# Latent attention's value products: a rounded part and a remainder side by side in one stationary tile, on one Trainium2 core

## The reference, cut to what matters

```python
    def attend(qblk):
        s = jnp.einsum('bqhd,bkhd->bhqk', qblk, k).astype(jnp.float32)
        p = jax.nn.softmax(s, axis=-1)
        return jnp.einsum('bhqk,bkhd->bqhd', p.astype(v.dtype), v)

    o = lax.map(attend, qb)
    o = o.transpose(1, 0, 2, 3, 4).reshape(B, S, B_HEADS * V_DIM)
    return o @ w_o
```

## Time and profile before

| | |
|---|---|
| median of 3 runs | 1272.54 us (1271.21 to 1272.92) |
| profiled execution, first to last instruction (span) | 1270.8 us |
| profiled execution, its own time | not given apart from its span |
| PE matmul busy | 1201.8 us, 95% of the span |
| DVE busy | 634.5 us, 50% |
| ACT busy | 370.1 us, 29% |
| POOL busy | 432.6 us, 34% |
| mean granted TensorE clock | 0.987 of full speed |
| dense attention, first scores to last values | 652.9 to 853.6 us |

### The profile page before, as it was taken

One profiled execution on the slowest core, in us unless ns is written; L12 is line 12 of the kernel. 1 busy time (PEld: TensorE's weight loads), 2 busy tenths in 40 slices (PEclk: granted clock), 3 DMA queues, 4 the chain that ended last, 5 costly groups with the idle time before them and its releaser, 6 DMA issues.

```text
span 1270.8 us, 19309 instructions
## 1 busy us (share of the span) xinstructions
PE 1201.8 (95%) x5804; PEld 996.6 (78%) x5804; DVE 634.5 (50%) x1055; ACT 370.1 (29%) x719; POOL 432.6 (34%) x474
## 2 busy tenths in 40 slices
PE   6988899999999999999989899999999999999996
PEld 4777787878888888888967677777788888888885
DVE  6666674444432544445476767745433432343432
ACT  3167672232210011011165656532222200101101
POOL 5455543433321323334242314215333321333341
PEclk9999999999999999999999999999999999999998
DMA  6211012233333233332201001013323432333331
GB/s 158 67 35 33 17 34 67 84 99 99 90 109 98 85 98 89 106 114 88 76 18 36 19 17 33 1 34 116 99 83 99 117 93 80 92 98 99 109 90 66
DMA packets 176473, 96.62 MB, mean 76 GB/s; under 512 B 8753, under 2 KB 173105, under 8 KB 176433
## 3 DMA queue, kind: packets, MB, share of 16 engines
q1 hardware_dynamic: 176432, 96.12, 25.9%
HBM read 94.01 MB, written 2.10 MB: 76 GB/s over the span
## 4 chain that ended last, share of the span: by engine, by line
PE 78%; DVE 8%; issue 6%; POOL 3%; ACT 3%; DMA 1%; DVEq 0%; ACTq 0%; SPq 0%; POOLq 0%
PE bank L975 25%; PE bank L977 24%; PE bank L976 24%; PE bank L1419 2%; POOL w_hi L436 1%; PE bank L1116 1%; DVE stat L2010 1%; POOL bias L516 1%; DVE w_lo L1501 1%; DMA w_raw<-in_a_w_qkv 1%; DVE bpt_lo L2015 1%; DVE apt_lo L1672 0%; ACT s_b L906 0%; DVE k_dup L1592 0%; DVE w_lo L1518 0%
## 5 line engine op out<-in xcount | busy, mean ns | idle before, releaser
L1501 DVE TENSOR_TENSOR w_lo<-w_raw,w_hi 128x1024 fp32r<-128x1024 f32 (+2 forms) x151 | 202.9, 1344 | 294.5 <-POOL w_hi L436 294.4
L436 POOL TENSOR_SCALAR w_hi<-w_raw 128x1024 fp32r<-128x1024 f32 (+3 forms) x159 | 184.5, 1160 | 414.8 <-PE bank L977 404.3
L975 PE MATMUL bank<-x_hi,w_lo 128*128 128x512 f32 x784 | 309.2, 394 | 8.4 <-DVE w_lo L1501 5.3
L976 PE MATMUL bank<-x_lo,w_hi 128*128 128x512 f32 x784 | 306.9, 391 | 0.0
L977 PE MATMUL bank<-x_hi,w_hi 128*128 128x512 f32 x784 | 306.6, 391 | 0.0
L975 PEld LDWEIGHTS bank<-x_hi,w_lo 128*128 128x128 f32 x784 | 147.9, 189 | 41.6 <-DVE w_lo L1501 7.4
L977 PEld LDWEIGHTS bank<-x_hi,w_hi 128*128 128x128 f32 x784 | 148.2, 189 | 31.4
L976 PEld LDWEIGHTS bank<-x_lo,w_hi 128*128 128x128 f32 x784 | 148.2, 189 | 29.4
L975 PE MATMUL bank<-f_hi,w_lo 128*128 128x512 f32 x352 | 137.8, 391 | 1.1 <-DVE f_lo L1782 1.1
L977 PE MATMUL bank<-f_hi,w_hi 128*128 128x512 f32 x352 | 137.0, 389 | 0.0
L976 PE MATMUL bank<-f_lo,w_hi 128*128 128x512 f32 x352 | 137.0, 389 | 0.0
(11 more groups left out here) (215 smaller groups left out, 1946.9 us busy)
## 6 DMA issues: line engine op xcount, KB each, us to landing
w_raw<-in_ffn_w_gu SPq DMA_DIRECT2D x88, 512.0 KB, 3.8
w_raw<-in_ffn_w_down SPq DMA_DIRECT2D x32, 704.0 KB, 4.4
w_raw<-in_a_w_qkv SPq DMA_DIRECT2D x12, 512.0 KB, 3.7
w_raw<-in_a_w_o SPq DMA_DIRECT2D x8, 512.0 KB, 3.5
w_raw<-in_b_w_o SPq DMA_DIRECT2D x8, 512.0 KB, 3.8
w_raw<-in_b_w_in SPq DMA_DIRECT2D x4, 672.0 KB, 4.0
w_raw<-in_b_w_uq SPq DMA_DIRECT2D x4, 576.0 KB, 4.0
x_n<-in_x SPq DMA_DIRECT2D x4, 512.0 KB, 5.0
```

The lines of the kernel that those rows point to most:

```text
L436: pool.tensor_scalar(split_part(w_hi, s, cols, kv), raw_part(s, cols, kv), 1.0, 1.0, ALU.mult, ALU.mult) \
L975: pe.matmul(o, ll, rh, start=start, stop=False)
L976: pe.matmul(o, lh, rl, start=False, stop=False)
L1501: dve.tensor_tensor(split_part(w_lo, s, cols, kv), raw_part(s, cols, kv), f(split_part(w_hi, s, cols, kv)), ALU.subtract) \
```

## The change

The value tile `bv` now holds, for each head and key block, the 64 columns of the rounded values and beside them the 64 columns of the remainder. A head takes two matmuls a key block, this tile x `bpt_lo` and this tile x `bpt_hi`. In the bank, partitions 0 to 63 then hold the rounded values' share and 64 to 127 the remainder's share (with low x low, which was left out before); their sum is the head's output. Heads 0 to 2 of a group use bank 5, head 3 bank 2. Per head ACT copies the lower half to `o_low` (`o_lower`) and DVE adds it to the upper half into a half of `o_sum` (`o_total`). After each odd head DVE copies `o_sum` to `ot_hi`, and POOL makes `ot_lo` from `o_sum` and `ot_hi` (`o_split`). `o_hi`, `o_lo` and the two memsets of the zero columns are gone. `wo_phase` waits for POOL's `o_ready` in place of DVE's `o_free`. The diff, its core:

```diff
@@ -201,11 +201,11 @@
             ("bk_hi", [P, HG, T], F32R), ("bk_lo", [P, HG, T], F32R)])
-        cq_hi, cq_lo, ckv_hi, ckv_lo, q_n, bv_hi, bv_lo, s_b, bpt_hi, bpt_lo, rope_a = region(scratch, [
+        cq_hi, cq_lo, ckv_hi, ckv_lo, q_n, bv, o_low, o_sum, s_b, bpt_hi, bpt_lo, rope_a = region(scratch, [
             ("cq_hi", [P, QL // P, T], F32R), ("cq_lo", [P, QL // P, T], F32R),
             ("ckv_hi", [P, KVL // P, T], F32R), ("ckv_lo", [P, KVL // P, T], F32R),
             ("q_n", [P, NT, HG * QK], F32),
-            ("bv_hi", [P, NT, 2, 3 * HD], F32R), ("bv_lo", [P, NT, 2, 3 * HD], F32R),
+            ("bv", [P, NT, HG, 2 * HD], F32R), ("o_low", [HD, T], F32), ("o_sum", [P, T], F32),
             ("s_b", [P, 2, HG, T], F32),
@@ -618,6 +620,14 @@
+            pool.memset(o_sum[:, 0:2], 0.0).then_inc(o_ready, 1)
+            def o_split(g, pair):
+                wait(pool, o_hi_ready, 4 * GROUPS + 2 * g + pair + 1)
+                pool.tensor_tensor(ot_lo[:, 2 * g + pair, :], o_sum[:], f(ot_hi[:, 2 * g + pair, :]), ALU.subtract) \
+                    .then_inc(o_ready, 1)
@@ -629,6 +639,9 @@
                         w_split_hi(C_B // 2 + 1 + g, 1, cols1, kv=cols0 == W_UQ)
+                    if u == 15:
+                        o_split(g, 0)
+                o_split(g, 1)
@@ -860,14 +873,12 @@
-            bv_hi_v = bv_hi[:].rearrange("p t a (s d) -> p (t a) s d", d=HD)
             def b_v_hi(g, i):
-                wait(act, o_done, 4 * GROUPS + 2 * g)
+                wait(act, o_done, 4 * GROUPS + HG * g)
                 wait(act, proj_done, U_BG * g + 6 + i + 1)
-                act.activation(bv_hi_v[:, 4 * i:4 * i + 4, ::2, :],
-                               banks[6 + i][:].rearrange("p (t s d) -> p t s d", t=4, s=2), ACT.Copy) \
+                act.activation(bv[:, 2 * i:2 * i + 2, :, 0:HD],
+                               banks[6 + i][:].rearrange("p (t h d) -> p t h d", t=2, h=HG), ACT.Copy) \
                     .then_inc(v_hi_ready, 1)
@@ -911,9 +920,11 @@
-                def o_hi(pair):
-                    wait(act, o_done, 4 * GROUPS + 2 * g + pair + 1)
-                    act.activation(ot_hi[:, 2 * g + pair, :], banks[5][:], ACT.Copy).then_inc(o_hi_ready, 1)
+                def o_lower(n):
+                    wait(act, o_free, O_B + HG * g + n)
+                    wait(act, o_done, 4 * GROUPS + HG * g + n + 1)
+                    act.activation(o_low[:], banks[5 if n < 3 else 2][HD:P, :], ACT.Copy).then_inc(o_low_ready, 1)
@@ -936,8 +947,8 @@
                             pt_hi(n, i)
-                        if n == 2:
-                            o_hi(0)
+                        if n:
+                            o_lower(n - 1)
                     else:
@@ -946,10 +957,11 @@
                                 b_k_hi(g + 1, i // 2)
+                        o_lower(2)
                         if not last:
                             for hd in range(HG):
                                 b_q_hi(hd, T_B + B_TG * g + 16)
-                        o_hi(1)
+                        o_lower(3)
@@ -1001,7 +1013,10 @@
                     pe.wait_ge(proj_free, u0 + s - 1)
-                    pe.wait_ge(o_free, O_A + 4 * (GROUPS - 1) if c0 == C_WOA else O_B + 2 * (GROUPS - 1))
+                    if c0 == C_WOA:
+                        pe.wait_ge(o_free, O_A + 4 * (GROUPS - 1))
+                    else:
+                        pe.wait_ge(o_ready, 2 * (GROUPS - 1) + 1)
                 for k in ks:
@@ -1196,9 +1211,9 @@
-            def wo_phase(c0, u0, o_count):
-                pe.wait_ge(o_free, o_count)
+            def wo_phase(c0, u0, o_landed, o_count):
+                pe.wait_ge(o_landed, o_count)
                 for s in range(2):
@@ -1405,6 +1420,8 @@
                     pe.wait_ge(exp_ready, S_B - S_A + before)
+                    if u == 2:
+                        pe.wait_ge(o_free, O_B + HG * g)
                     q = (slice(0, QK), n, slice(qb * P, (qb + 1) * P))
@@ -1431,14 +1448,14 @@
                             pe.wait_ge(proj_free, U_B + U_BG * g + U_BG)
-                    if i == 0 and n % 2 == 0:
-                        pe.wait_ge(o_free, O_B + 2 * g + n // 2)
-                    v = (slice(None), i, n // 2, slice(HD, HD + P) if n % 2 else slice(0, P))
-                    p = (slice(None), n % 2, i, slice(None))
-                    last_ = product(banks[5][:], bv_hi[v], bv_lo[v], bpt_hi[p], bpt_lo[p],
-                                    n % 2 == 0 and i == 0, n % 2 == 1 and i == NT - 1)
-                    if n % 2 and i == NT - 1:
+                    if i == 0 and n < 3:
+                        pe.wait_ge(o_free, O_B + HG * g + n)
+                    o = banks[5 if n < 3 else 2][:]
+                    v = bv[:, i, n, :]
+                    pe.matmul(o, v, bpt_lo[:, n % 2, i, :], start=i == 0, stop=False)
+                    last_ = pe.matmul(o, v, bpt_hi[:, n % 2, i, :], start=False, stop=i == NT - 1)
+                    if i == NT - 1:
                         last_.then_inc(o_done, 1)
@@ -1968,14 +1983,11 @@
-            bv_hi_v = bv_hi[:].rearrange("p t a (s d) -> p (t a) s d", d=HD)
-            bv_lo_v = bv_lo[:].rearrange("p t a (s d) -> p (t a) s d", d=HD)
             def b_v_lo(g, i):
                 wait(dve, v_hi_ready, GROUPS + 2 * g + i + 1)
-                dve.tensor_tensor(bv_lo_v[:, 4 * i:4 * i + 4, ::2, :],
-                                  banks[6 + i][:].rearrange("p (t s d) -> p t s d", t=4, s=2),
-                                  f(bv_hi_v[:, 4 * i:4 * i + 4, ::2, :]), ALU.subtract).then_inc(proj_free, 1)
+                dve.tensor_tensor(bv[:, 2 * i:2 * i + 2, :, HD:2 * HD],
+                                  banks[6 + i][:].rearrange("p (t h d) -> p t h d", t=2, h=HG),
+                                  f(bv[:, 2 * i:2 * i + 2, :, 0:HD]), ALU.subtract).then_inc(proj_free, 1)
@@ -2015,10 +2027,17 @@
-                def o_lo(pair):
-                    wait(dve, o_hi_ready, 4 * GROUPS + 2 * g + pair + 1)
-                    dve.tensor_tensor(ot_lo[:, 2 * g + pair, :], banks[5][:], f(ot_hi[:, 2 * g + pair, :]),
-                                      ALU.subtract).then_inc(o_free, 1)
+                def o_total(n):
+                    if n % 2 == 0:
+                        wait(dve, o_ready, 2 * g + n // 2 + 1)
+                    wait(dve, o_low_ready, HG * g + n + 1)
+                    rows = slice(n % 2 * HD, (n % 2 + 1) * HD)
+                    dve.tensor_tensor(o_sum[rows, :], banks[5 if n < 3 else 2][0:HD, :], o_low[:], ALU.add) \
+                        .then_inc(o_free, 1)
+                    if n % 2:
+                        wait(dve, o_free, O_B + HG * g + n + 1)
+                        dve.tensor_copy(ot_hi[:, 2 * g + n // 2, :], o_sum[:]).then_inc(o_hi_ready, 1)
@@ -2058,9 +2077,10 @@
                             pt_lo(2, 3)
-                            o_lo(0)
-                            if not last:
-                                b_rotate_q(g + 1, 0)
+                        if n:
+                            o_total(n - 1)
+                        if n == 2 and not last:
+                            b_rotate_q(g + 1, 0)
                     else:
@@ -2068,12 +2088,13 @@
                                 b_rotate_q(g + 1, 1)
+                        o_total(2)
                         if not last:
                             for hd in range(HG):
                                 b_q_lo(hd, T_B + B_TG * g + 16)
                                 if hd == 0:
                                     b_k_lo(g + 1, 1)
-                        o_lo(1)
+                        o_total(3)
```

More of the change, by code:

```diff
@@ L87 @@
 O_B = O_NORM1 + 1
-O_NORM3 = O_B + 2 * GROUPS
+O_NORM3 = O_B + HG * GROUPS
 S_A = 16
@@ L249, in build @@
         o_free = sem("o_free")
+        o_low_ready = sem("o_low_ready")
+        o_ready = sem("o_ready")
         x_hi_ready = sem("x_hi_ready")
@@ L888, in _ @@
             b_q_hi(3, T_BPRE + 6)
-            act.wait_ge(vec_consts, 8)
             act.wait_ge(krope_pool, 4)
@@ L1271, in ffn_half @@
                     sum_partitions(norms[4])
-            wo_phase(C_WOA, U_WOA, O_A + 4 * GROUPS)
+            wo_phase(C_WOA, U_WOA, o_free, O_A + 4 * GROUPS)
             ffn_half(0, 0, norms[1])
@@ L1489, in _ @@
             b_group(GROUPS - 1, True)
-            wo_phase(C_WOB, U_WOB, O_B + 2 * GROUPS)
+            wo_phase(C_WOB, U_WOB, o_ready, 2 * GROUPS + 1)
             ffn_half(1, 0, norms[3])
@@ L1865, in _ @@
             angles()
-            for t in (bv_hi, bv_lo):
-                dve.memset(f(t[:, :, :, HD:2 * HD]), 0.0).then_inc(vec_consts, 1)
             ffn_half(0, 1, norms[2], W_LAT, mid=cosines)
```

## The result

| | us |
|---|---|
| before, median of 4 runs in this comparison | 1272.73 (1271.21 to 1275.31) |
| changed kernel, median of 4 runs | 1281.14 (1278.68 to 1363.18) |
| ratio of the undisturbed runs | 1.0058, 95% interval 1.0040 to 1.0076 |
| profiled execution of the changed kernel | 1278.68, span 1276.9, mean clock 0.980 (before 0.987) |

By the ratio the change costs 7.4 us. The forecast was no change at 1273.9 us, with 1265 to 1279 as its range; the measured median lies above it. One run, of 1363.18 us at a mean clock of 0.847, is disturbed and not in the ratio; the median of the other three is 1279.91 us, above the range too.

A forecast was written before the change was run, and what follows sets the result against it. PE was busy over 90%, but waits for ACT's exponential and DVE's `bpt_lo` set the pace in places. Span 1270.8 - 0.1 + 1.5 (clock) = 1272.2; with 1.7 from span to median, 1273.9 us, range 1265 to 1279.

The forecast's parts named there:

- PE's saving: Value products, two matmuls for three: of 3.7 us a group 1.4 is kept; 2.1 us in the last group.
- Late start of round 2: Unit 12's maximum on DVE stands behind `o_total(0)`, so round 2 of each group starts 0.7 us later.
- Late start of a group: At a group's start the first maximum waits for head 3's addition and the copy to `ot_hi`: +0.5 us.
- The tail of head 3: Head 3's products alternate with query transposes; `bq_lo` comes later, so only about 0.15 us of the saving is kept.
- The last group: Dense attention's last group, projection matmuls following: -2.1 us saved, +0.7 for round 2, together -1.4 us.
- Prices: Durations taken for new rows: copy to `ot_hi` 0.4 us (else 0.69), half-height ACT row 0.593, POOL subtraction 1.29.
- The projection's chain: Before the output projection `ot_lo` comes through ACT, DVE and POOL: 3.27 us instead of 1.38, or +1.9 us.
- The third rival: POOL's subtractions delay DVE by 1.3 us once a group where it has no slack: 5.2 us, 1277.6; chance 0.10.
- The clock: More PE idle time in the groups brings one more stretch at half clock, 1.5 us; how many follow was left open.
- The second rival: Clock drops everywhere: four more drops, 6.0 us, plus 1.2 for a dearer copy, giving 1279.6 us; chance 0.24.
- The forecast's -0.1: Sum without the clock: -0.6 us for groups 0 to 2, -1.4 for the last, +1.9 before the projection.

The follow-up runs named there:

- e1: Kernel before the change with the first of three value matmuls left out and no new rows on ACT, DVE or POOL: 1268.76 us, ratio 0.9966.
- e8: Kernel before with that value matmul left out, plus matmuls with unread results before units 3, 11 and 15: 1264.62 us, ratio 0.9942.
- e3: Changed kernel plus matmuls with unread results where PE waits (before units 3, 11, 15 and the output projection): 1271.79 us, ratio 0.9989.
- e4: Kernel before the change plus matmuls with unread results where PE waits (3 before units 3 and 11): 1270.06 us, ratio 0.9978.
- e2: Changed kernel with a third matmul in each value product (remainder pass issued twice), so PE's work is as before: 1285.05 us, ratio 1.0097.
- e11: Changed kernel plus 7 matmuls with unread results before the output projection only: 1280.08 us, ratio 1.0053.
- e5: Changed kernel with some sums and a lower-half copy moved later, and POOL making the second pair's `ot_hi` in groups 0 to 2: 1270.28 us, ratio 0.9983.

## Why the prediction was wrong

- **PE's saving**: right. Of 3.7 us a group 1.4 arrives (e1: 1.41, e8 the same), 1.8 of the 2.1 in the last. The rest goes into the transposes' bank and DVE's `bq_lo`, as named, and into one wait that was not named, the query transpose's for `bpt_lo` (2.2 us in e1 as well).
- **Late start of round 2**: right, 0.7 forecast, 0.74 measured.
- **Late start of a group, "+0.5 us"**: too small; it measured 0.87. The steps missed that `bq_lo` holds DVE 0.1 us longer; the copy waits 0.19 for the addition before it, where 0.1 was taken, and 0.12 of idle follows it. The tail of head 3, "kept: about 0.15", kept nothing (group 2: the group is 0.41 us late at its end, and 0.40 at the start of head 3's products). Together 0.6 us a group.
- **The last group, "-1.4"**: too large. From its first scores to its last value product it takes 44.54 us in e3 and 44.88 in e4, both at full clock: 0.34 less. The steps give 0.9 less (the 1.4, and 0.5 back for its late start). Group 0 can't be read so, since its clock fell in both.
- **Prices**: the copy took 0.427 us (taken 0.4, against 0.69), the half-height ACT row 0.596, POOL's subtraction 1.28, each as taken:

```profile
L2040 DVE CAST ot_hi<-o_sum x8: 426/427/429, 692.8 to 858.7; 128x512 f32 x6, 128x512 fp32r<-128x512 f32 x2
L628 POOL TENSOR_TENSOR ot_lo<-o_sum,ot_hi x8: 1262/1282/1438, 693.5 to 859.2; 128x512 f32 x6, 128x512 fp32r<-128x512 f32 x2
```

- **The projection's chain, "+1.9"**: right. ACT to PE:

```profile
857.34 0.59 ACT L927 ACTIVATE o_low<-bank 64x512 f32<-64x512 f32 x1 [2.36 <-PE bank L1457]
857.96 0.68 DVE L2036 TENSOR_TENSOR o_sum<-bank,o_low 64x512 f32<-64x512 f32 x1 [2.21 <-ACT o_low L927]
858.68 0.43 DVE L2040 CAST ot_hi<-o_sum 128x512 fp32r<-128x512 f32 x1
859.19 1.26 POOL L628 TENSOR_TENSOR ot_lo<-o_sum,ot_hi 128x512 fp32r<-128x512 f32 x1 [10.25 <-DVE ot_hi L2040]
860.50 0.50 PE L987 MATMUL bank<-ot_hi,w_lo 128*128 128x512 f32 x1 [1.91 <-POOL ot_lo L628]
```

  3.16 us from ACT's start to PE's, against 1.38 in the earlier trace rows.
- **The third rival, "DVE is held longer"**: the hold was there, in a place with slack. In each of groups 0 to 2 one small rotation row of DVE started 0.2 us after POOL's first subtraction and ended only after it:

```profile
746.37 1.38 DVE L1916 TENSOR_TENSOR rs_t<-q_n,sin_n 128x128 f32<-128x128 f32 x1
746.17 1.44 POOL L628 TENSOR_TENSOR ot_lo<-o_sum,ot_hi 128x512 f32 x1 [2.86 <-DVE ot_hi L2040]
```

  The same row takes 0.28 us before the change. Of these 1.1 us nothing is seen to reach PE: its transposes of round 3 wait for nothing, and DVE is idle for 0.86 us two rows later, until ACT's `bk_hi` comes.
- **The clock, "I count one more drop of 1.5 us"**: this is the step that failed. Against 1.5 us the runs show 6.0 (the change costs 7.4 without and 1.4 with filling; the interval is about 3 to 9). In the profiled run there are three new drops: at the start of group 1, of group 3, where it alone costs 2.4 us, and behind the projection's wait. The second rival had the repeated drops, at 1279.6 us and 0.24. That its number fits is in part luck: it held 1.2 us for a dearer copy, which did not come, and nothing for the late starts and the last group, which did. I had taken group 2's full clock for a sign that most groups would hold; the same group drops in e2 and in e11. The rule of the Trainium skill that the prediction named (TensorE: Matmul & The Clock Gate, "What's actually happening": half rate is the default, activity releases it) was the better guide; e3 fits it, 47 idle-time matmuls for 8.8 us.

A second way to the clock's share, an estimate: e5's twelve runs of one program go from 1267.56 us at a mean clock of 0.989 to 1274.40 at 0.977, 0.57 us for each 0.001. The three runs of the changed kernel in the ratio had 0.978 to 0.980, the kernel before a median of 0.986 to 0.987 in the experiments: 0.008 less, or 4.6 us. Both ways lie well above 1.5.

With filling, at nearly equal clocks, the change costs 1.4 us (e3 against e4, within 2). The forecast's -0.1, with the 0.6 for each of groups 1 and 2 and the nearly 0.6 of the last, comes to 1.7.

## What to carry to other kernels

Two matmuls in place of three are worth what the next wait leaves: here 1.4 of 3.7 us a group, and the price was new rows ahead of the row that paced PE. Put such rows behind the pacing one (e5: 9.6 us), even where their engine is half idle. Where PE waits often for a microsecond, count the granted clock as a cost of every new wait, and do not take one group of one profile that kept its clock as a sign that the others will. Try a few thrown-away matmuls in the waits: here they left the full-clock groups as long as they were and gave 2.8 us on the kernel before and 8.8 on the changed one.

## What the runs showed of the hardware

**The clock.** No wait of PE in the changed kernel's dense attention is longer than 1.9 us. The drops at the start of groups 1 and 3 came after waits of 0.7, 0.4 to 0.5 and 1.3 us close together. In group 2 nearly the same waits (0.73, 0.41, 1.29) brought none in the profiled run; in e11's, all three groups dropped. A stretch at half clock cost 1.4 us in round 1 of group 1 before the change (51.66 us, against 50.29 for group 2) and 2.4 at the start of group 3 after it; the two in the changed kernel's group 1 cost 2.0 together (52.71 against 50.70), the two in a group of e11 3.6.

**DVE and POOL.** A DVE row of 128x128 with two SBUF sources took 1.38 us beside a POOL subtraction of two SBUF tensors that had started 0.2 us before it, and 0.28 without. The copy of 128x512 within SBUF took 0.427 us into float32 and into fp32r alike.
